# A hybrid encoder step on one Trainium2 core: the router of each token tile moved between the steps of the output projection, and ScalarE's work reordered where the running streams begin

## The chip, the cores and the metric

The kernel runs on one core of one Trainium2 chip. The metric is the device time of one execution in microseconds (us), the median of several runs. Everything is float32; large products are split into a high and a low part that TensorE takes as three float32r matmuls.

## What is computed

The reference is one layer over 512 prompt tokens and 8 running streams of 16 tokens, 640 tokens of width 1024. Cut to what matters here:

```python
x = x + concat(ao, go) @ w_out                 # ao: attention heads, go: gated linear attention
h = rms_norm(x, gain2)
g_logits = h @ w_group + b_group               # 4 groups
e_logits = h @ w_erouter + b_erouter           # 32 experts
# top group, top two experts in it, softmax weights
y = y + combine[:, e] * (silu(h @ w_gate[e]) * (h @ w_up[e])) @ w_down[e]
```

The attention of the prompt sees its own keys; that of a stream sees 512 cached keys and its 16 new ones.

## The kernel before

The 640 tokens are five tiles of 128 rows: tiles 0 to 3 are the prompt, tile 4 holds the eight streams. Each engine has one program, written out by hand, and the engines meet at semaphores: `then_inc` counts up, `wait_ge` holds the engine's queue until the count is reached. An engine works its instructions off in the order in which they are written, so a wait holds back all that stands behind it.

The place of the change begins where the prompt's attention ends (about 300 us) and ends where the mixture of experts begins (about 415 us):

- **The streams.** For each stream b the key cache and the value cache arrive in three buffers (SyncE, L505 and L513). TensorE computes scores (`d_scores`, L2007), VectorE the negated maximum (`d_max`, L1401), ScalarE two exponentials (`d_exps`, L931 and L933), VectorE a small table of factors (`d_comb`, L1410), TensorE transposes and combines (`d_pt`, L2023), ScalarE copies the result out of PSUM (`d_pts`, L942 and L943), TensorE multiplies with the values (`d_pv`, L2034). The loop runs over b with TensorE at score b, transpose b-2 and product b-3 in one turn.
- **The weights of the output projection** are halved into high and low parts between the streams' steps: `wo_high` (ScalarE, L790, 2048 columns at a time) and `wo_low` (VectorE, L1237). Both halves must be there before the first projection of this stage.
- **Projection of the attention part.** `a_step(s)` stands for three steps of tile i = s // 3: transposes of the mixed heads (TensorE L2052), split into high and low (`a_high` on ScalarE L954, `a_low` on VectorE L1417), and two projections of 512 columns, 12 matmuls each (L1955 to L1957). VectorE adds each half to the residual X (`a_add`, L1435). Steps 0 to 6 stand in the streams' turns, 7 to 14 behind them.
- **Router of tile i.** Eight transposes of X (`h2_tr`, TensorE L2093), two copies out of PSUM (`h2_out`, ScalarE L995), sum of squares (`sumsq`, VectorE L1467), root (`std_out`, ScalarE L1000), reciprocal and logits (`logits`, VectorE L1472 and L1475), the router's eight matmuls of 36 columns (`router`, TensorE L2104). `hn_out` (ScalarE L1007) writes the normed tile into one of two buffers `hn`, and GpSimd stores it to memory (L683), from where the experts gather their rows. `sumsq` writes its squares, which nobody reads, into the same buffer: for tile i of 2 and more it waits until the store of tile i-2 has landed (`st_hn`).
- **Choice of experts.** `pick` and `place` on VectorE for tiles 0 to 2, then for 3 and 4, with rank matmuls on TensorE, make the list of rows. GpSimd waits for the list and for all five stores, then gathers 128 rows for each of 16 pairs of experts (L712).
- **Experts.** Each has 3 MB of weights, in six buffers. SyncE loads experts 0 to 2 when the last stream's product is done (L516 and L519), 3 and 4 when the last projection is done, and the sixth when the first two gathers have landed; the others wait for a buffer.

ScalarE's `osq`, four squares and a root for the prompt's heads, needs another table of functions than the exponentials; each change of table is an instruction of its own (ACT_TABLE_LOAD). Two places say what sets the order around the change:

```python
            def sumsq(i):
                dve.wait_ge(x2_ready, 2 * NT + 2 * i + 2)
                if i >= 2:
                    dve.wait_ge(st_hn[i % 2], 16 * (i // 2))
```

```python
            sp.wait_ge(out_done, 4 * NT)
            for e in (3, 4):
                gate_up_of(e)
                down_of(e)
```

Of the kernel before, what the change touches and what calls it, by code (L numbers as in the profile page):

```python
# [24 lines left out]
P = 128  # L25
D = 1024
DC = D // P
NT = 5
NP = 4
CHUNK = 64  # L30
NB = 8
# [41 lines left out]
def build(nc, x, cache_kt, cache_v, state, w_main, w_ga, w_a2b, w_out, cols, k_gain, lam, w_r, b_r,  # L73
          w_gu, w_dn, y_out, k_out, v_out, sp_out, ss_out, hn_dram, ye_dram):
    ctx = ExitStack()
    with ctx:
# [653 lines left out]
        def _(act):  # L730
# [235 lines left out]
            d_exps(1)  # L966
            osq(NP - 1)
# [14 lines left out]
            for h in range(H):  # L982
                ins = act.activation(junk[:, h, :], bank[5][:, h * P:(h + 1) * P], ACT.Square,
                                     accum_out=sso[:, NP, h:h + 1])
            ins.then_inc(o_sq, 1)
            act.wait_ge(o_sq, NT)
            act.activation(ro[:, NP, 0:H], sso[:, NP, 0:H], ACT.Sqrt, bias=epsc[:, 0:1],
                           scale=1.0 / DV).then_inc(ostd, 1)

            def h2_out(i):  # L990
                for q in range(2):
# [87 lines left out]
        def _(dve):  # L1079
# [363 lines left out]
            d_max(0)  # L1443
            turn(NI + 2)
            d_max(1)
            d_comb(0)
            g_step(NS - 1)
            dve.wait_ge(ostd, 2)
            dve.reciprocal(ro[:, 0:NP, 0:H], ro[:, 0:NP, 0:H]).then_inc(ro_ready, 1)
            dve.wait_ge(x2_ready, 2 * NT)  # L1450
            for b in range(2, NB + 3):
                if b < NB:
                    d_max(b)
                if 5 <= b:
                    a_step(b - 5)
                if 1 <= b <= NB:
                    d_comb(b - 1)
                if b in (2, 3):
                    wo_low(1, b - 2)
# [844 lines left out]
```

## Time and profile before

| | |
|---|---|
| median of 3 runs | 695.02 us (694.23 to 702.57) |
| profiled execution, its own time | 696.28 us |
| its span in the trace | 694.5 us |
| mean granted TensorE clock | 0.922 of full |
| PE busy | 572.1 us (82%) |
| VectorE (DVE), ScalarE (ACT), GpSimd (POOL) busy | 251.4, 191.7, 88.2 us |
| moved by DMA | 166.46 MB, mean 240 GB/s |

The span runs from the first to the last instruction; 1.8 us of the execution's time lie outside it. A long busy time of an engine alone says little here: first TensorE sets the pace, then a web of short waits between engines, then the loading of the experts' weights.

### The profile page before, as it was taken

What the parts mean: (1) busy time and instruction counts of PE and PEld (TensorE: products, weight loads), DVE (VectorE), ACT (ScalarE), POOL (GpSimd) and SP (SyncE); (2) the same over time, 40 slices, a digit from 0 to 9 for tenths busy, and PEclk for the clock granted to TensorE, in tenths of its full rate; (3) what the DMA queues carried; (4) which work ended last, traced back from release to release, by engine and by line L of the source; (5) the groups of instructions that cost most, each with busy time, mean ns of one, the idle gap of its engine ahead of it and who ended that gap; (6) DMA issues with size and microseconds to landing.
All of it is one profiled execution on the core that took longest, in us unless ns stands there. A gap on an engine that the chain in (4) does not pass through costs nothing.

```text
span 694.5 us, 8437 instructions
## 1 busy us (share of the span) xinstructions
PE 572.1 (82%) x3375; PEld 377.7 (54%) x3375; DVE 251.4 (36%) x536; ACT 191.7 (28%) x439; POOL 88.2 (13%) x124
## 2 busy tenths in 40 slices
PE   5999999999989889769978837999968787878730
PEld 4878787777878667647866733444423333333200
DVE  3732347743593566535332671011100000100006
ACT  4441725232324444544332220111101111111110
POOL 4000000011862100010000111112111111110010
PEclk9999999999999899998997957999989999999885
DMA  8211221011343850068467286999999999999338
GB/s 300 68 62 60 96 88 61 1 62 61 121 176 135 333 212 1 1 255 322 152 267 319 98 376 225 424 423 427 422 424 425 423 425 424 426 424 428 144 138 357
DMA packets 24344, 166.46 MB, mean 240 GB/s; under 512 B 4752, under 2 KB 5328, under 8 KB 11120
## 3 DMA queue, kind: packets, MB, share of 16 engines
q1 hardware_dynamic: 17264, 146.36, 52.6%
q0 software_dynamic: 6320, 16.92, 6.3%
q10 hardware_dynamic: 720, 2.62, 0.9%
q8 instruction: 28, 0.46, 0.3%
q14 instruction: 12, 0.10, 0.0%
HBM read 154.74 MB, written 17.43 MB: 248 GB/s over the span
## 4 chain that ended last, share of the span: by engine, by line
PE 58%; DMA 24%; DVE 5%; ACT 5%; issue 4%; POOL 2%; SPq 1%; POOLq 0%; ACTq 0%; DVEq 0%
DMA egu<-in_w_gu 18%; PE twin L2183 11%; PE twin L1696 7%; PE twin L1698 7%; PE twin L1697 7%; PE twin L2203 3%; PE twin L1955 3%; PE twin L1956 3%; PE twin L1957 3%; DMA yg<-ye_dram 2%; PE twin L2034 2%; DMA hn_dram<-hn 1%; DVE xsT L1631 1%; DMA X<-in_x 1%; PE twin L2023 1%
## 5 line engine op out<-in xcount | busy, mean ns | idle before, releaser
L2183 PE MATMUL twin<-egu,xsT 128*64 128x512 f32 x512 | 130.0, 666 | 39.9 <-DMA egu<-in_w_gu 34.1
L2183 PEld LDWEIGHTS twin<-egu,xsT 128*64 128x64 f32 x512 | 46.4, 152 | 113.4 <-issue 113.4
L1696 PE MATMUL twin<-wH,hH 128*128 128x512 f32 x240 | 97.5, 406 | 0.0
L1698 PE MATMUL twin<-wH,hL 128*128 128x512 f32 x240 | 94.0, 392 | 0.0
L1697 PE MATMUL twin<-wL,hH 128*128 128x512 f32 x240 | 93.9, 391 | 0.0
L1637 DVE TENSOR_TENSOR hs<-sil,twin 128x256 f32<-128x256 f32 x16 | 6.7, 421 | 166.3 <-ACT sil L1034 166.3
L2203 PE MATMUL twin<-edn,hTs 128*64 128x512 f32 x256 | 58.1, 592 | 1.1 <-ACT hTs L1038 1.1
L1034 ACT ACTIVATE sil<-twin 128x256 f32<-128x256 f32 x16 | 6.1, 384 | 169.9 <-PE twin L2183 169.9
L1696 PEld LDWEIGHTS twin<-wH,hH 128*128 128x128 f32 x240 | 45.4, 189 | 10.7 <-issue 1.8
L1698 PEld LDWEIGHTS twin<-wH,hL 128*128 128x128 f32 x240 | 45.2, 188 | 9.9
L1697 PEld LDWEIGHTS twin<-wL,hH 128*128 128x128 f32 x240 | 45.4, 189 | 8.4
L1101 DVE SCALAR_TENSOR_TENSOR wL<-win,colt,wH 128x512 fp32r<-128x512 f32 x48 | 40.3, 901 | 5.4 <-ACT wH L742 5.4
L2203 PEld LDWEIGHTS twin<-edn,hTs 128*64 128x64 f32 x256 | 21.5, 137 | 34.1 <-issue 32.8
L1631 DVE TENSOR_TENSOR xsT<-twin,colt 128x512 f32<-128x512 f32 x32 | 20.7, 686 | 50.1 <-PE twin L2172 50.1
L712 POOL DMA_INDIRECT xs<-hn_dram,idx x16 | 16.1, 1007 | 177.9 <-ACT ysb L1049 153.1
L742 ACT ACTIVATE wH<-win,colt 128x512 fp32r<-128x512 f32 x48 | 30.7, 716 | 9.1 <-DMA win<-in_w_main 9.1
L1049 ACT ACTIVATE ysb<-twin 128x512 f32<-128x512 f32 x32 | 17.4, 595 | 49.5 <-PE twin L2203 49.5
L879 ACT ACTIVATE E<-twin,nm 128x128 f32<-128x128 f32 (+3 forms) x32 | 16.6, 524 | 30.4 <-DVE nm L1326 30.4
L2172 PEld LDWEIGHTS twin<-ident,xs 128*128 128x128 f32 x128 | 14.4, 146 | 18.7 <-issue 12.2
L639 POOL TENSOR_TENSOR zV<-zK 128x512 f32<-128x512 f32 x5 | 5.3, 1053 | 145.2 <-ACT zK L766 145.2
L2172 PE MATMUL twin<-ident,xs 128*128 128x128 f32 x128 | 18.4, 289 | 6.5 <-DMA xs<-hn_dram,idx 6.5
L1955 PE MATMUL twin<-wH,mixH 128*128 128x512 f32 x40 | 19.7, 492 | 4.4 <-DVE mixL L1351 2.4
(312 smaller groups left out, 823.4 us busy)
## 6 DMA issues: line engine op xcount, KB each, us to landing
egu<-in_w_gu SPq DMA_DIRECT2D x32, 2048.0 KB, 35.1
edn<-in_w_dn SPq DMA_DIRECT2D x32, 1024.0 KB, 39.2
win<-in_w_main SPq DMA_DIRECT2D x12, 1024.0 KB, 5.0
Kc<-in_cache_kt SPq DMA_DIRECT2D x8, 1024.0 KB, 9.9
Vc<-in_cache_v SPq DMA_DIRECT2D x8, 1024.0 KB, 6.9
X<-in_x SPq DMA_DIRECT2D x10, 512.0 KB, 8.1
yg<-ye_dram SPq DMA_DIRECT2D x5, 1024.0 KB, 9.1
hn_dram<-hn POOLq DMA_DIRECT2D x5, 512.0 KB, 2.9
```

The costliest lines, as they stand in the source:

```text
L742: act.activation(wH[k][:, o], win[k][:, o], ACT.Copy, scale=g1[:, 4 * k + s:4 * k + s + 1]).then_inc(wH_ready, 1)
L1101: dve.scalar_tensor_tensor(out=wL[k][:, o], in0=win[k][:, o], scalar=g1[:, 4 * k + s:4 * k + s + 1], in1=wH[k][:, o].bitcast(F32), op0=ALU ...
L1631: dve.tensor_tensor(xsT[q][:, 4 * hf:4 * hf + 4, :], bank[hf][:, :].rearrange("p (c s) -> p c s", c=4), bc(g2[:, 4 * hf:4 * hf + 4], [P, 4 ...
L1696: pe.matmul(bank[i][:, :], hH[:, d, i, :], wH[k][:, cs], start=(d == 0), stop=False)
L1697: pe.matmul(bank[i][:, :], hH[:, d, i, :], wL[k][:, cs], start=False, stop=False)
L1698: ins = pe.matmul(bank[i][:, :], hL[:, d, i, :], wH[k][:, cs], start=False, stop=(d == DC - 1))
L1955: pe.matmul(out, xH[i % 2][:, c, :], w_high, start=(c == 0), stop=False)
L1956: pe.matmul(out, xH[i % 2][:, c, :], w_low, start=False, stop=False)
L1957: ins = pe.matmul(out, xL[i % 2][:, c, :], w_high, start=False, stop=(c == H - 1))
L2172: ins = pe.transpose(bank[hf][:, c * P:(c + 1) * P], xs[q][:, (4 * hf + c) * P:(4 * hf + c + 1) * P], ident[:, :])
L2183: ins = pe.matmul(bank[2 + q][CAP * j:CAP * j + CAP, :], xsT[q][:, c, j * CAP:(j + 1) * CAP], egu[places[j]][:, c, :], start=(c == 0), sto ...
L2203: ins = pe.matmul(bank[4 + 2 * q + hf][CAP * j:CAP * j + CAP, :], hTs[q][:, f, j * CAP:(j + 1) * CAP], edn[places[j]][:, f, hf * 512:(hf + ...
```

## The change

It moves instructions and alters a few waits; no instruction of arithmetic is added or removed.

1. **ScalarE where the streams begin.** The copy-out of stream 0 (`d_pts(0)`) and the exponentials of stream 2 come ahead of `osq(3)` and its root. Copies-out stand one turn earlier in the loop, `wo_high` and VectorE's `wo_low` one turn later (b in 3 and 4 in place of 2 and 3), behind `d_pts` where they stood ahead of it.
2. **Tile 0's router in the streams' turns.** TensorE's `h2_tr(0)` goes into the turn b = 8, `router(0)` into b = 9, VectorE's `sumsq(0)` into b = 8.
3. **Interleaving.** Behind the streams the projections of the next tile are placed between the router's steps, so that a router matmul comes at least one projection after the transposes that it needs.

```diff
             d_exps(1)
+            d_pts(0)
+            d_exps(2)
             osq(NP - 1)
...
-            for b in range(2, NB + 3):
+            for b in range(3, NB + 2):
                 if b in (5, 8):
                     a_high((b - 5) // 3)
                 if b < NB:
                     d_exps(b)
-                if b in (2, 3):
-                    wo_high(1, b - 2)
-                if 2 <= b < NB + 2:
-                    d_pts(b - 2)
-            a_high(2)
-            act.wait_ge(d_pv_done, NB)
...
+                d_pts(b - 2)
+                if b in (3, 4):
+                    wo_high(1, b - 3)
...
+            h2_out(0)
             std_out(0)
-            h2_out(0)
+            a_high(2)
+            stream_squares()
+            h2_out(1)
+            std_out(1)
+            hn_out(0)
             a_high(3)
-            std_out(1)
-            h2_out(1)
-            hn_out(0)
+            hn_out(1)
+            h2_out(2)
+            std_out(2)
             a_high(4)
-            hn_out(1)
-            std_out(2)
-            h2_out(2)
             hn_out(2)
+            h2_out(3)
             std_out(3)
-            h2_out(3)
             hn_out(3)
+            h2_out(4)
             std_out(4)
-            h2_out(4)
             hn_out(4)
```

`stream_squares` is the four squares and the root of the streams' heads, which stood behind `a_high(2)` before. On VectorE:

```diff
+            for b in range(3, NB + 3):
...
+                if b in (3, 4):
+                    wo_low(1, b - 3)
+                if b == NB:
+                    sumsq(0)
+            logits(0)
...
             a_step(6)
-            stream_ao()
+            sumsq(1)
+            stream_copy()
             a_step(7)
+            stream_norm()
+            a_step(9)
+            logits(1)
             a_step(8)
-            sumsq(0)
-            a_step(9)
-            logits(0)
+            sumsq(2)
             a_step(10)
-            sumsq(1)
-            logits(1)
+            a_step(11)
             a_step(12)
-            a_step(11)
-            sumsq(2)
             sumsq(3)
             logits(2)
             pick(0, LATE[0])
             a_step(13)
-            logits(3)
             a_step(14)
             sumsq(4)
+            logits(3)
             place(0, LATE[0], 1)
```

And on TensorE, whose projections and routers behind the streams then read:

```diff
+                if b == NB:
+                    h2_tr(0)
+                if b == NB + 1:
+                    router(0)
+
+            h2_tr(1)
             a_step(7)
+            a_step(9)
+            router(1)
             a_step(8)
-            h2_tr(0)
-            a_step(9)
-            router(0)
-            h2_tr(1)
             a_step(10)
-            router(1)
+            h2_tr(2)
+            a_step(11)
             a_step(12)
-            a_step(11)
-            h2_tr(2)
             router(2)
             h2_tr(3)
             a_step(13)
+            a_step(14)
             router(3)
-            a_step(14)
             ranks(1)
             h2_tr(4)
             router(4)
```

On ScalarE, where the streams begin (E and enew are a stream's exponentials, PT its copy-out, junk the squares of `osq`, wH and woH the high halves of `wo_high`), the kernel before has:

```order
L894 ACTIVATE junk,sso<-zQ 128x128 x3
L969 ACT_TABLE_LOAD
L969 ACTIVATE ro<-sso,epsc 128x4x4 [waits o_sq]
L931 ACT_TABLE_LOAD [waits cb_ready,pt_done]
L931 ACTIVATE E,ds<-twin,nm 128x512 [waits nm_ready]
L933 ACTIVATE enew,ds<-twin,nm 128x16
L790 ACTIVATE wH<-win 128x2048 [waits out_done,ld_win0]
L942 ACTIVATE PT<-twin 128x512 [waits o_done,d_pt_done]
L943 ACTIVATE PT<-twin 128x128
```

and the changed kernel in the same place:

```order
L942 ACTIVATE PT<-twin 128x512 [waits o_done,d_pt_done]
L943 ACTIVATE PT<-twin 128x128
L931 ACTIVATE E,ds<-twin,nm 128x512 [waits cb_ready,pt_done,nm_ready]
L933 ACTIVATE enew,ds<-twin,nm 128x16
L894 ACTIVATE junk,sso<-zQ 128x128 [waits ao_ready]
L894 ACTIVATE junk,sso<-zQ 128x128 x3
L971 ACT_TABLE_LOAD
L971 ACTIVATE ro<-sso,epsc 128x4x4 [waits o_sq]
L931 ACT_TABLE_LOAD [waits cb_ready,d_pt_done]
L931 ACTIVATE E,ds<-twin,nm 128x512 [waits nm_ready]
L933 ACTIVATE enew,ds<-twin,nm 128x16
L942 ACTIVATE PT<-twin 128x512 [waits o_done,d_pt_done]
```

The first copy-out (PT) and one pair of exponentials moved ahead of the squares and of both table loads; the first `wo_high` moved behind the second copy-out, which is the last row shown.

On VectorE behind the streams, at the sums of squares of tiles 2 and 3 (ISA hn,ss is `sumsq`, Lg the logits, X an addition to the residual, mixL an `a_low`), the kernel before has:

```order
L1467 ISA hn,ss<-X 128x1024 [waits mT_done,x2_ready]
L1467 ISA ss 128x1
L1472 RECIPROCAL r<-st 128x1 [waits std1]
L1475 SCALAR_TENSOR_TENSOR Lg<-twin,r,br 128x36 [waits rstd1,lg_done]
L1423 SCALAR_TENSOR_TENSOR mixL<-twin,ag,mixH 128x4x32 [waits mH_ready]
L1423 SCALAR_TENSOR_TENSOR mixL<-twin,ag,mixH 128x4x32 x3
L1435 TENSOR_TENSOR X<-X,twin 128x512 [waits out_done]
L1467 ISA hn,ss<-X 128x1024 [waits st_hn0,x2_ready]
L1467 ISA ss 128x1
L1467 ISA hn,ss<-X 128x1024 [waits st_hn1,x2_ready]
```

and the changed kernel:

```order
L1463 SCALAR_TENSOR_TENSOR Lg<-twin,r,br 128x36 [waits rstd1,lg_done]
L1441 TENSOR_TENSOR X<-X,twin 128x512 [waits out_done]
L1455 ISA hn,ss<-X 128x1024 [waits st_hn0,x2_ready]
L1455 ISA ss 128x1
L1441 TENSOR_TENSOR X<-X,twin 128x512 [waits out_done] x2
L1429 SCALAR_TENSOR_TENSOR mixL<-twin,ag,mixH 128x4x32 [waits mH_ready]
L1429 SCALAR_TENSOR_TENSOR mixL<-twin,ag,mixH 128x4x32 x3
L1455 ISA hn,ss<-X 128x1024 [waits st_hn1,x2_ready]
L1455 ISA ss 128x1
L1460 RECIPROCAL r<-st 128x1 [waits std1]
```

The sum of squares that waits for the first store (`st_hn0`) now stands ahead of two additions and of the streams' `a_low`.

## Rows read from the trace of the kernel before

**Rows 1.** Busy time by stretch: us, each engine (x instructions), granted clock, DMA share, GB/s
```profile
327.00:352.60 25.60, 25.58 (x327) 19.86 (x325) 6.20 (x16) 5.60 (x17) 0.00 (x0) 1.00 0.39 148
352.60:397.80 45.20, 35.97 (x183) 30.93 (x183) 19.42 (x59) 14.53 (x32) 4.04 (x6) 0.85 0.63 256
440.00:642.00 202.00, 168.00 (x770) 70.54 (x766) 22.65 (x40) 24.36 (x53) 25.18 (x25) 0.93 1.01 424
```

**Rows 2.** Chain that ended last, 340 to 425 us: start, us, what
```profile
403.91 10.09 DMA hn_dram<-hn
...
414.86 4.16 DMA xs<-hn_dram,idx
```

**Rows 3.** Timeline of TensorE: start, us, line, operation, [idle before <- releaser]
```profile
313.71 2.05 PE L2023 MATMUL twin<-Cb,E 128*128 128x128 f32 x8 [5.76 <-ACT PT L943]
...
326.45 0.50 PE L1955 MATMUL twin<-wH,mixH 128*128 128x512 f32 x1
...
354.14 0.50 PE L1955 MATMUL twin<-wH,mixH 128*128 128x512 f32 x1 [1.56 <-DVE mixL L1417]
...
359.72 1.03 PE L2093 MATMUL twin<-ident,X 128*128 128x128 f32 x8
...
375.20 1.98 PE L2104 MATMUL twin<-wr,h2T 128*128 128x36 f32 x16 [3.22 <-ACT h2T L995]
```

**Rows 4.** Timeline of ScalarE
```profile
308.79 1.28 ACT L931 ACT_TABLE_LOAD   x1
310.08 0.69 ACT L931 ACTIVATE E<-twin,nm 128x512 f32<-128x512 f32 x1
...
311.01 1.90 ACT L790 ACTIVATE wH<-win 128x2048 fp32r<-128x2048 f32 x1
312.81 0.59 ACT L942 ACTIVATE PT<-twin 128x512 f32<-128x512 f32 x1
...
352.62 0.69 ACT L954 ACTIVATE mixH<-twin,ag 128x512 fp32r<-128x512 f32 x1 [5.22 <-PE twin L2052]
...
355.65 0.30 ACT L987 ACTIVATE ro<-sso,epsc 128x4 f32<-128x4 f32 x1
...
361.99 1.06 ACT L995 ACTIVATE h2T<-twin 128x512 f32<-128x512 f32 x2
```

**Rows 5.** Timeline of VectorE
```profile
312.94 2.37 DVE L1237 TENSOR_TENSOR wL<-win,wH 128x2048 fp32r<-128x2048 f32 x1 [1.72 <-ACT wH L790]
315.24 0.69 DVE L1401 TENSOR_REDUCE nm<-twin 128x1 f32<-128x528 f32 x1
...
387.52 0.17 DVE L1501 TENSOR_REDUCE gmax<-Lg 128x3 f32<-128x12 f32 x1
...
393.13 0.69 DVE L1435 TENSOR_TENSOR X<-X,twin 128x512 f32<-128x512 f32 x1
...
397.77 1.22 DVE L1467 CUSTOM_DVE_ANT_0 hn<-X 128x1024 f32<-128x1024 f32 x1
...
412.97 0.17 DVE L1612 SCALAR_TENSOR_TENSOR idx<-twin,none 128x17 int32<-128x17 f32 x1
```

**Rows 6.** The tile hn: durations of one in ns (min/median/max), and its stores
```profile
L1007 ACT ACTIVATE hn<-X,r x5: 1146/1148/1162, 375.0 to 402.5; 128x1024 f32<-128x1024 f32 x5
...
DMA to landing us min/median/max: 2.9/2.9/10.1
```

**Rows 7.** Timeline of SyncE: issues of the experts' loads
```profile
352.09 0.33 SPq L516 DMA_DIRECT2D egu<-in_w_gu  x1
...
397.04 0.33 SPq L516 DMA_DIRECT2D egu<-in_w_gu  x1
```

**Rows 8.** DMA queues from 408 to 412 us: packets, MB, share of 16 engines
```profile
q1 hardware_dynamic: 85, 1.34, 79.3%
q0 software_dynamic: 84, 0.34, 20.9%
```

**Rows 9.** DMA issues of the whole run: number, median us to landing
```profile
ye_dram<-ysb,dst POOLq DMA_INDIRECT x16, 14.4
```

More of the change, by code:

```diff
@@ L975, in _ @@
                     d_exps(b)
-                if b in (2, 3):
-                    wo_high(1, b - 2)
-                if 2 <= b < NB + 2:
-                    d_pts(b - 2)
-            a_high(2)
-            act.wait_ge(d_pv_done, NB)
[L982 to L988, printed above, removed]
+                d_pts(b - 2)
+                if b in (3, 4):
+                    wo_high(1, b - 3)
             def h2_out(i):
+                if i == 0:
+                    act.wait_ge(d_pv_done, NB - 2)
                 for q in range(2):
@@ L1441, in a_step @@
                     a_add(s // 3, s % 3 - 1)
[L1443 to L1459, printed above, removed]
             def sumsq(i):
@@ L1476, in logits, with stream_copy, stream_norm @@
                                          in1=br[:, :], op0=ALU.mult, op1=ALU.add).then_inc(lg_ready, 1)
-            def stream_ao():
+            d_max(0)
+            turn(NI + 2)
+            d_max(1)
+            d_comb(0)
+            g_step(NS - 1)
+            d_max(2)
+            d_comb(1)
+            dve.wait_ge(ostd, 2)
+            dve.reciprocal(ro[:, 0:NP, 0:H], ro[:, 0:NP, 0:H]).then_inc(ro_ready, 1)
+            dve.wait_ge(x2_ready, 2 * NT)
+            for b in range(3, NB + 3):
+                if b < NB:
+                    d_max(b)
+                if 5 <= b:
+                    a_step(b - 5)
+                if b <= NB:
+                    d_comb(b - 1)
+                if b in (3, 4):
[3 more added lines that the diff above has]
+            logits(0)
+            def stream_copy():
                 dve.wait_ge(o_sq, NT)
                 dve.tensor_copy(z(C_Q, NP), bank[5][:, :]).then_inc(ao_ready, 1)
+            def stream_norm():
                 dve.wait_ge(ostd, 3)
@@ L2069, in a_step @@
                 project_out(bank[7 if i < 2 or hf == 0 else 4][:, :], i, hf, 0, out_done)
-            turn(NI + 1)
-            d_scores(0)
-            turn(NI + 2)
-            d_scores(1)
-            for b in range(2, NB + 3):
-                if b < NB:
-                    d_scores(b)
-                if 2 <= b < NB + 2:
-                    d_pt(b - 2)
-                if b >= 3:
-                    d_pv(b - 3)
-                if b >= 4:
-                    a_step(b - 4)
             def h2_tr(i):
@@ L2100, in router @@
                     pe.wait_ge(lg_ready, i - 1)
+                elif i:
+                    pe.wait_ge(d_pt_ready, 2 * NB)
                 else:
                     pe.wait_ge(gains_ready, 1)
+                    pe.wait_ge(d_e_ready, 2 * NB)
                 for c in range(DC):
@@ L2138, in tables @@
                     ins.then_inc(tab_done, 1)
+            turn(NI + 1)
+            d_scores(0)
+            turn(NI + 2)
+            d_scores(1)
+            for b in range(2, NB + 3):
+                if b < NB:
+                    d_scores(b)
+                if 2 <= b < NB + 2:
+                    d_pt(b - 2)
+                if b >= 3:
+                    d_pv(b - 3)
+                if b >= 4:
+                    a_step(b - 4)
+                if b == NB:
[3 more added lines that the diff above has]
+            h2_tr(1)
             a_step(7)
+            a_step(9)
+            router(1)
             a_step(8)
-            h2_tr(0)
-            a_step(9)
-            router(0)
-            h2_tr(1)
             a_step(10)
-            router(1)
+            h2_tr(2)
+            a_step(11)
             a_step(12)
-            a_step(11)
-            h2_tr(2)
             router(2)
```

11 lines of the change are left out of this document (10 added, 1 removed).

## The prediction, made before the run

> **What bounds the kernel now.** I read the end first, then back to the place of the change. From 440 to 642 us the DMA engines are full (share 1.01, 424 GB/s) while TensorE waits for weights [rows 1]: that stretch lasts as long as its bytes take. It starts rigidly behind the first gathers, since SyncE's next loads wait for two gathers and for the buffers that the first pairs of experts free. The chain of waits shows what releases the first gather, at 414.86: the landing of the last store of `hn`, which took 10.09 us [rows 2], while the list of rows was ready at 413.1, 0.9 us sooner [rows 5]. So what counts is how soon the list and the stores are there, and whatever they gain the whole tail gains.
>
> Behind the last stream, from 352.6 to 397.8 us, TensorE is busy for 36.0 of 45.2 us, at a mean granted clock of 0.85 of 2.4 GHz [rows 1]. Its timeline shows why: projection, transposes, then a wait for a copy-out, 1.56 us before the projection of tile 2 and 3.22 us before the router of tile 1 [rows 3]. In the streams' turns before it, from 327 on, TensorE is busy for 25.58 of 25.60 us at full clock [rows 1]. At their beginning it waits 5.76 us for ScalarE's first copy-out [rows 3], which stands behind two table loads and a `wo_high` of 1.90 us [rows 4].
>
> I take two marks from before: t0 = 352.6, when ScalarE starts `a_high(2)` [rows 4], and S4 = 397.8, when VectorE starts the last sum of squares [rows 5]. From S4 to the gather it takes 17.1 us.
>
> **1. ScalarE where the streams begin: 0.6 us lost.** `d_pts(0)` no longer waits for the squares, so the 5.76 us go; but what is late next is the projection's weights. The two exponentials and copies put ahead delay the table loads' end from 310.1 to about 312.9 (0.85 for the copy, 0.95 for the exponentials, 1.05 waiting for the first transpose). Then follow one after the other, because each waits for the one before on the other engine: exponentials 0.95 and copy 0.85, `wo_high` 1.90, `wo_low` 2.37, maximum 0.69, exponentials 0.95, copy 0.85, `wo_high` 1.90, `wo_low` 2.3, maximum 0.69, and an `a_low` of 0.75 [rows 4, 5]: 14.2 us, so `a_step(1)` starts at 327.1 in place of 326.45 [rows 3]. The maximum of the next stream is queued behind each `wo_low` on VectorE, as before. SyncE's loads of keys and values are released no later than before and hide here. Bounds: 5.8 us gained if the weights don't decide, about 3 lost if more is late.
>
> The Trainium skill (ScalarE: Activation LUTs, section "What ACT_TABLE_LOAD costs") counts about 1.38 us of drain on top of 1.28 for each switch of tables. The trace has 1.28 and the exponential 0.01 us behind the load [rows 4]; by the page the two switches would end 2.8 us later and the time would be 688.7, but the row shows nothing of it.
>
> **2. Tile 0's router in the turns: 3.0 us lost on TensorE there.** TensorE is dense from 327 on, so eight transposes (1.03) and the router (1.98) have no cover [rows 3]. What they wait for is ready: ScalarE's two copies of `h2_out(0)` (1.06 [rows 4]) lie beside the projection between them.
>
> The granted clock is a cost that the order doesn't show. After the wait of 5.76 us four transposes ran at half clock, 2.05 us [rows 3]. The changed kernel spreads the same idle time over waits up to about 327, so the first dense block may run at half: between nothing and 3.4 us; I take 1.2, the first 2.4 us of a projection at half. So t0 becomes 352.6 + 0.6 + 3.0 + 1.2 = 357.4.
>
> **3. Interleaving: from t0 to S4 31 us in place of 45.2.** Two projections in a row take 5.6 us (354.14 to 359.72 [rows 3]). TensorE waits once more, some 0.7 us for `a_low(2)` beside the transposes of tile 1; after that each wait has a projection in front of it. Six projections (16.8), two routers (4.0), two sets of transposes of X (2.1) and two of heads (1.1) from 1.6 on end the last projection at t0 + 25.6. This is not the end of it: VectorE needs `pick` (5.6 us, 387.52 to 393.13 [rows 5]) after the sum of squares of tile 2 and 3, and these wait for stores.
>
> Now the stores. Before, three of five landed in 2.9 us; the last, issued at 403.9 beside the loads of experts 3 and 4 (issued from 397.04 on), took 10.1 [rows 2, 6, 7]. In the changed kernel the first three meet a load: experts 0 to 2 are issued 0.5 us before t0 as now [rows 7], and 9.4 MB at 424 GB/s with two stores among them last until about t0 + 25.8. ScalarE reaches the store of tile 0 after `a_high(2)` 0.69, squares and root (in all 2.05, the 3.33 us from 352.62 to 355.95 less a table load that now comes earlier), `h2_out(1)` 1.06, `std_out` 0.3, `hn_out(0)` 1.15 and 0.3 until the issue [rows 4, 6]: t0 + 5. At 10 us it lands at 15. Tile 1's store queues behind it: under load its queue moved 0.34 MB in 4 us [rows 8], so 0.52 MB take 6, until 21. `sumsq(3)` waits for this (it could start at 19). Then 1.22 for it, 1.4 for reciprocal and `hn_out(2)`, 0.3 to the issue: tile 2's store leaves at 24. `pick` ends at 28.3, two additions at 29.7, and `sumsq(4)` needs that store. It lands at 26.9 if it finds the engines free, at 34 if it meets load throughout. It is issued when the first load has under 2 us left, and experts 3 and 4 begin about 27, so it should find a gap: S4 between 29.7 and 34, taken at 31, nearer to the 2.9 row.
>
> The Trainium skill (DMA: Bandwidth & Descriptors, section "Anatomy of one DMA — SWDGE (gpsimd) path") gives 2.0 us plus the bytes at 436 GB/s for a transfer issued by GpSimd, 3.2 us by estimate for one store. Three of the five stores agree (2.9), the one under load doesn't (10.1) [rows 6]; taken for all of them the rule is the first rival below.
>
> **4. From S4 to the gather: 0.25 us lost.** `hn_out(3)` (1.15) now stands ahead of `h2_out(4)`, while the list instead of the last store releases the gather (0.9 gained). GpSimd's stores leave earlier, and experts 3 and 4 load while `pick` and `place` run, as before.
>
> **Sum.** S4 = 357.4 + 31 = 388.4, 9.35 earlier; less 0.25 is 9.1 us. The profiled execution took 696.28, its span plus 1.8, and would take 687.2; it was 1.26 above the median of the runs, so the forecast for the median is 695.02 - 9.1 = 685.9. Its own range: with no clock cost and S4 at 29.7, 683.4; with 3.4 and 34, 691.1. Two per cent, about what can be told from no change, is 13.9 us, so this counts as no change.
>
> **Rivals.**
> - *Stores land in 2.9 us even under load.* Then `sumsq(2)` and `sumsq(3)` never wait; the last projection ends at 25.6, additions follow `pick` at 27.6, and S4 is 27.7: 682.6. For it: three of five stores. Against: the one store that met a load [rows 2, 6], and that the two queues' packets alternate, 84 and 85 in 4 us, while the loads' are four times as large (1.34 MB to 0.34) [rows 8]. Chance 0.10.
> - *The weights don't hold the streams back.* Then the 5.76 us are gained, t0 is 6.4 earlier: 679.5. For it: the wait stands in the chain [rows 3]. Against: a `wo_low` has to end before `a_step(1)` and nothing shortens that chain. Chance 0.13.
> - *Slower: the stores take longer than that one did.* Two of them stand in a row before S4, and one in between, so S4 = 14 + 2x for a store of x us; it decides from x = 13.1 on. GpSimd's scatters on the same queue, all under full load, take 14.4 in the median [rows 9]: then S4 is 42.8, at 400.2 us, and the time 697.7. Against: they are scattered rows, and the plain store beside a load took 10.1. Chance 0.07.
>
> **How the numbers follow.** The forecast has a chance of 0.67, and 0.03 is left for what I don't see. Below 681.1 lie the second rival, a third of the first and the forecast's lower edge: faster by over 2% 0.20. Slower by over 2%, past 708.9, is only in what I don't see: 0.03. The rest, 0.77, is within 2%. The range of 8 in 10 goes from 678.0, which takes in the second rival with a little more, to 692.5, the forecast's upper bound and a little of what lies beyond.
>
> **What would show it.** Right: VectorE's third and fourth sums of squares wait for a DMA of `hn`, with stores of about 10 us after t0; `a_step(1)` starts near 327; TensorE is nearly dense from t0 to its last projection, at full clock; the gather starts near 405.8. Wrong: the copy-outs of the streams follow each other without the `wo_high` between them deciding (second rival), sums of squares that start behind an addition (first), or an S4 past 397 (third).

## The result, and the profile after

The changed kernel takes 683.55 us (median of 4 runs, 682.82 to 684.23), the kernel before, run beside it, 694.62 us. The ratio is 0.9863, 95% interval 0.9829 to 0.9896: 11.1 us less, which is within 2%. Here and below a ratio compares the fast executions alone, while medians and ranges take in all. The forecast was 685.9 us, 9.1 us less, with a range of 678.0 to 692.5.

The profiled execution took 683.54 us, its span 681.7. To compare executions I use one more mark, M: the start of ScalarE's exponentials of stream 0, just ahead of all that the change touches. It is at 299.44 us before and 299.82 in the changed kernel, and what lies ahead of it is nobody's gain or loss here. Timeline of ScalarE, changed kernel (start, us, line, operation, [idle before <- releaser]); the last row is the mark t0 of the prediction, at 352.62 before [rows 4]:

```profile
299.82 0.69 ACT L931 ACTIVATE E<-twin,nm 128x512 f32<-128x512 f32 x1 [4.90 <-DVE nm L1407]
...
310.18 1.28 ACT L971 ACT_TABLE_LOAD   x1
311.47 0.31 ACT L971 ACTIVATE ro<-sso,epsc 128x16 f32<-128x16 f32 x1
...
356.85 0.69 ACT L954 ACTIVATE mixH<-twin,ag 128x512 fp32r<-128x512 f32 x1 [4.34 <-PE twin L2064]
```

The busy time by stretch, columns as in [rows 1]: from 0.75 us ahead of t0 to 2.8 us behind S4, then t0 to the end of the last projection, then the place where the first projection of the turns runs.

```profile
356.10:390.00 33.90, 28.96 (x177) 25.03 (x170) 19.72 (x60) 12.23 (x29) 3.52 (x6) 0.92 0.97 398
356.85:381.35 24.50, 23.81 (x139) 20.48 (x137) 13.25 (x37) 10.77 (x27) 2.92 (x5) 1.00 0.99 402
326.00:330.00 4.00, 3.30 (x8) 2.67 (x9) 1.12 (x4) 1.69 (x6) 0.00 (x0) 0.57 0.54 223
```

Behind t0 TensorE is now busy 29.0 of 33.9 us (36.0 of 45.2 before), and the DMA share there is 0.97 in place of 0.63. Up to the end of its last projection it is nearly dense, and at full clock. Its timeline, where the waits of [rows 3] stood:

```profile
314.40 1.06 PE L2019 MATMUL twin<-Kc,qbd 128*32 128x512 f32 x8 [3.53 <-DMA Kc<-in_cache_kt]
...
326.70 0.79 PE L1967 MATMUL twin<-wH,mixH 128*128 128x512 f32 x1 [2.73 <-DVE mixL L1423]
...
358.38 0.50 PE L1967 MATMUL twin<-wH,mixH 128*128 128x512 f32 x1 [0.69 <-DVE mixL L1423]
...
385.53 1.97 PE L2091 MATMUL twin<-ident,X 128*128 128x128 f32 x8 [1.75 <-DVE X L1441]
390.71 3.63 PE L2105 MATMUL twin<-wr,h2T 128*128 128x36 f32 x16 [3.21 <-ACT h2T L989]
```

From 358.38 until the last projection ends it doesn't wait at all: of the 1.56 us of before 0.69 are left, and the 3.22 are gone. The waits of VectorE have moved to DMA. Its timeline (the first three rows are the sums of squares of tiles 2, 3 and 4; the last is the list of rows, at 412.97 before [rows 5]):

```profile
371.73 1.23 DVE L1455 CUSTOM_DVE_ANT_0 hn<-X 128x1024 f32<-128x1024 f32 x1 [4.63 <-DMA hn_dram<-hn]
...
376.77 1.23 DVE L1455 CUSTOM_DVE_ANT_0 hn<-X 128x1024 f32<-128x1024 f32 x1 [1.28 <-DMA hn_dram<-hn]
...
387.20 1.23 DVE L1455 CUSTOM_DVE_ANT_0 hn<-X 128x1024 f32<-128x1024 f32 x1 [1.73 <-DMA hn_dram<-hn]
...
404.01 0.17 DVE L1624 SCALAR_TENSOR_TENSOR idx<-twin,none 128x17 int32<-128x17 f32 x1
```

S4, the last of the three, is at 387.20, t0 + 30.35. The chain that ended last goes through two of these stores (start, us, what):

```profile
363.71 1.16 ACT hn L1001
364.87 0.29 issue
365.16 11.48 DMA hn_dram<-hn
376.77 1.23 DVE hn L1455
378.11 1.16 ACT hn L1001
379.27 0.28 issue
379.56 7.50 DMA hn_dram<-hn
387.20 1.23 DVE hn L1455
```

The view of the tile `hn` has for the five stores, where before it had 2.9, 2.9 and 10.1 [rows 6]:

```profile
DMA to landing us min/median/max: 7.5/10.2/11.5
```

GpSimd's first gather now waits for the list, not for a store:

```profile
405.13 1.10 POOL L712 DMA_INDIRECT xs<-hn_dram,idx  x1 [10.83 <-DVE idx L1624]
```

So the 12.8 us of the two spans (694.5 and 681.7) divide as follows. M is 0.38 later. The gather comes 105.31 us after M in place of 115.42: 10.11 gained. From the gather to the end of the span it is 276.57 us in place of 279.64: 3.07 gained, of which 2.95 are one group of matmuls, the gate and up product of the last pair of experts, during which the granted clock is 0.70 before and 1.00 changed. TensorE's timeline, before and changed:

```profile
647.74 10.04 PE L2183 MATMUL twin<-egu,xsT 128*64 128x512 f32 x32 [4.15 <-DMA egu<-in_w_gu]
```

```profile
638.14 7.09 PE L2200 MATMUL twin<-egu,xsT 128*64 128x512 f32 x32 [2.45 <-DMA egu<-in_w_gu]
```

### The profile page after: what moved, and what is told of

It is laid out like the page before. It is cut to its first block, busy times and chain, and to the rows that moved or that the text cites. A ratio compares the mean times of both kernels' runs of the same rounds, so it can differ in the third digit from the quotient of the medians.

```text
span 681.7 us, 8438 instructions
## 1 busy us (share of the span) xinstructions
PE 563.9 (83%) x3375; PEld 373.0 (55%) x3375; DVE 250.5 (37%) x536; ACT 191.3 (28%) x439; POOL 88.2 (13%) x124
## 4 chain that ended last, share of the span: by engine, by line
PE 55%; DMA 26%; DVE 6%; ACT 6%; issue 3%; POOL 2%; SPq 1%; POOLq 0%; ACTq 0%; DVEq 0%
DMA egu<-in_w_gu 19%; PE twin L2200 11%; PE twin L1708 7%; PE twin L1710 7%; PE twin L1709 7%; PE twin L2220 4%; DMA hn_dram<-hn 3%; PE twin L1967 3%; DMA yg<-ye_dram 2%; PE twin L1968 2%; PE twin L1969 2%; DMA X<-in_x 1%; DVE xsT L1643 1%; PE twin L1903 1%; POOL zK L646 1%
## 5 line engine op out<-in xcount | busy, mean ns | idle before, releaser
L2200 PE MATMUL twin<-egu,xsT 128*64 128x512 f32 x512 | 128.4, 659 | 38.6 <-DMA egu<-in_w_gu 32.8
L1710 PEld LDWEIGHTS twin<-wH,hL 128*128 128x128 f32 x240 | 45.2, 188 | 9.8
```

What stands on the lines that cost most here:

```text
L1710: ins = pe.matmul(bank[i][:, :], hL[:, d, i, :], wH[k][:, cs], start=False, stop=(d == DC - 1))
L2200: ins = pe.matmul(bank[2 + q][CAP * j:CAP * j + CAP, :], xsT[q][:, c, j * CAP:(j + 1) * CAP], egu[places[j]][:, c, :], start=(c == 0), sto ...
```

## The experiments

My theory: the interleaving (part 3) gains, and what then sets S4 are the stores of `hn` under the loads of experts 0 to 2; part 1 is neutral but for the clock; part 2 costs TensorE what it holds. Rivals: parts 1 and 2 carry the gain; the waits for stores are slack; the load isn't what makes the stores slow. The marks of all profiled executions (us, worked out from the timelines; "tail" is from the first gather to the end of the span, "last pair" its gate and up product). A mark comes from one execution. The medians were taken at four times, and the kernel before, run beside them, took 694.62 us (first two rows), 692.55 (one tile after the other, part 2 undone, part 1 undone, own scratch), 692.51 (changed again, two experts first, late loads, three edits) and 693.11 (the rest), so times are compared by their ratios:

| kernel | M | t0 - M | S4 - t0 | gather - M | tail | last pair | profiled | median |
|---|---|---|---|---|---|---|---|---|
| before | 299.44 | 53.18 | 45.15 | 115.42 | 279.64 | 10.04 | 696.28 | 694.62 |
| changed | 299.82 | 57.03 | 30.35 | 105.31 | 276.57 | 7.09 | 683.54 | 683.55 |
| changed, again | 298.72 | 55.61 | 29.24 | 102.80 | 278.68 | 8.49 | 682.08 | 683.67 |
| one tile after the other | 298.86 | 55.61 | 44.04 | 116.62 | 280.22 | 10.08 | 697.56 | 695.53 |
| part 2 undone | 298.95 | 53.02 | 33.22 | 104.18 | 280.07 | 8.78 | 685.25 | 687.96 |
| part 1 undone | 299.87 | 55.73 | 29.22 | 103.68 | 279.15 | 8.61 | 684.74 | 681.84 |
| part 3 alone | 297.99 | 52.97 | 37.48 | 108.39 | 279.72 | 8.65 | 687.96 | 687.36 |
| own scratch | 295.87 | 55.61 | 27.29 | 100.83 | 276.80 | 7.09 | 675.57 | 681.73 |
| two experts first | 295.93 | 55.62 | 28.45 | 102.37 | 278.50 | 7.09 | 678.73 | 684.68 |
| late loads | 299.60 | 57.05 | 27.30 | 102.70 | 289.60 | 8.78 | 693.85 | 690.16 |
| three edits | 300.00 | 55.82 | 27.30 | 101.94 | 279.56 | 10.00 | 683.46 | 679.48 |
| three edits, again | 296.48 | 55.58 | 27.29 | 101.83 | 279.49 | 8.64 | 679.74 | 679.74 |
| and last store free | 296.56 | 55.61 | 27.29 | 99.41 | 282.13 | 8.79 | 680.07 | 680.21 |

### The changed kernel again

No edit.

> The changed kernel once more, unaltered, as the yardstick for the runs beside it and for how far its executions scatter. My theory of the tail (from the first gather to the end of the span 276.6 us, of which 7.1 are the last pair's gate and up product at full clock, and 3 us more where that product falls into a low clock): the time is 683 to 687, each execution near one of two levels some 2 to 3 us apart, and in the profiled one the tail less the last pair's product is 269.5 within 1.5. Rival (the shorter tail of the first profile belongs to the change): every execution within 1 us of 683.5.

683.67 us (682.08 to 687.35, 6 runs), ratio 0.9884 (0.9842 to 0.9926). The tail less the last pair's product is 270.19, as expected; the product took 8.49 us this time. The rival, a shorter tail by the change, falls: the same kernel has either. The two levels of time that I expected don't appear, the six times lie spread. The gather starts 1.13 us behind the list of rows, 1.12 in the first profile; here it is the last store that is named as its releaser, so list and store come nearly together. t0 is 1.42 us nearer to M than in the first profile, and the stretches show why: the low clock, which met the first projection there (0.57 from 326 to 330), lies between 314 and 318 here, behind a wait of 3.52 us for a key cache. The first profile has that wait too (3.53 us), with the clock at 1.00 behind it.

```profile
326.00:330.00 4.00, 4.00 (x31) 2.65 (x30) 0.35 (x2) 0.61 (x2) 0.00 (x0) 1.00 0.30 117
314.00:318.00 4.00, 4.00 (x54) 3.20 (x50) 2.49 (x2) 1.48 (x1) 1.08 (x2) 0.62 1.01 426
```

### One tile after the other

TensorE's order (VectorE's and ScalarE's likewise):

```diff
-            h2_tr(1)
             a_step(7)
+            a_step(8)
             a_step(9)
-            router(1)
-            a_step(8)
+            h2_tr(1)
             a_step(10)
-            h2_tr(2)
+            router(1)
+            a_step(12)
             a_step(11)
-            a_step(12)
+            h2_tr(2)
             router(2)
```

> The changed kernel with parts 1 and 2 kept, but behind the last stream the order of before on TensorE, VectorE and ScalarE: each tile's projection, transposes and router one after the other. My theory (the interleaving is what gained): from t0, where ScalarE copies the heads of tile 2, to S4, the last sum of squares, it takes again 42 to 45 us in place of 30.35, the gather starts 10 to 12 us later than 405.13, and the time is 693 to 697. Rival (parts 1 and 2 carry half of the gain): t0 stays at about 356.9 and the time rises by 3 to 6 us only, to 687 to 690. If the 3 us that the tail gained beyond the gather belong to the interleaving, the tail from the gather's start to the end of the span is 3 us longer as well; if they are chance, it may be either length.

695.53 us (692.94 to 698.02, 12 runs), ratio 1.0044 (1.0019 to 1.007): without part 3 nothing of the gain is left, and 0.4% is lost. S4 - t0 is 44.04, nearly the 45.15 of before, and the gather comes 11.3 us after that of the first profile of the changed kernel (both from M), released by a store as before:

```profile
415.48 1.10 POOL L712 DMA_INDIRECT xs<-hn_dram,idx  x1 [10.29 <-DMA hn_dram<-hn]
```

### Part 2 undone

```diff
-                if b == NB:
-                    h2_tr(0)
-                if b == NB + 1:
-                    router(0)
 
-            h2_tr(1)
+            h2_tr(0)
             a_step(7)
+            router(0)
+            h2_tr(1)
             a_step(9)
             router(1)
```

ScalarE's copies and VectorE's logits of tile 0 go back with them; VectorE's `sumsq(0)` stays in the turns.

> The changed kernel without part 2: tile 0's transposes and router stand behind the streams again, the transposes ahead of the projection of tile 2 and the router behind its first half; the rest of the interleaving is kept. My theory: t0 is 3.0 us earlier (the TensorE time of transposes and router), but TensorE does that work after t0, and the store of tile 0 leaves about 2 us later, so S4 and the gather come 2 us later (0 to 4) and the time is 684 to 687.5. Rival (the stores don't set S4, TensorE does): S4 and the time as in the changed kernel, within 0.5 us. Second rival (the move only cost): the 3.0 us come back and the time is 680 to 681.

687.96 us (684.47 to 691.25, 12 runs), ratio 0.9937 (0.9909 to 0.9965). t0 is 2.6 us earlier, S4 - t0 4.0 us longer than in the second profile of the changed kernel, the gather 1.4 later. The direction is the theory's; the median lies 0.5 us above its range and some 4 above that of the changed kernel, while the marks show 1.4. The interval lies apart from the first one of the changed kernel and overlaps the second a little. The profiled execution, 685.25, is one of the quicker. Why the others are slower the next run suggests.

### Part 3 alone

Part 2 undone as above, and part 1 as below.

> The kernel before with the interleaving alone: parts 1 and 2 undone, so that only the order behind the last stream is that of the changed kernel. My theory (the interleaving gains what is gained, parts 1 and 2 move it by less than 2 us together): the gather comes 103 to 105.5 us after the first exponentials of the streams, in place of 115.4 before and 102.8 to 105.3 changed, and the time is 684 to 689. Rival (the interleaving pays only with tile 0's router out of the way): the gather at 108 or later and a time of 690 and more.

687.36 us (679.65 to 691.70, 6 runs), ratio 0.9858 (0.9798 to 0.9918), too wide an interval to tell it from the changed kernel or from part 2 undone. The time is within my range, but the gather comes at M + 108.39, where the rival put it, 4.2 us behind the run with part 2 alone undone, though t0 is the same. Most of the difference is one store. With part 2 undone the third store left at 379.24 and SyncE's load of expert 3 at 379.75, 0.5 us behind it; the last sum of squares met no wait. The view of the DMA issues, 378 to 387 us, has for this one store (KB each, us from issue to landing):

```profile
hn_dram<-hn POOLq DMA_DIRECT2D x1, 512.0 KB, 3.7
```

With part 3 alone both left together (SyncE, then GpSimd):

```profile
378.83 0.33 SPq L516 DMA_DIRECT2D egu<-in_w_gu  x1
```

```profile
378.78 0.53 POOL L683 DMA_DIRECT2D hn_dram<-hn  x1 [15.22 <-ACT hn L999]
```

and VectorE waited until the store landed. The view of the DMA issues, 376 to 384 us, and VectorE's timeline:

```profile
hn_dram<-hn POOLq DMA_DIRECT2D x1, 512.0 KB, 9.5
```

```profile
388.44 1.23 DVE L1453 CUSTOM_DVE_ANT_0 hn<-X 128x1024 f32<-128x1024 f32 x1 [3.76 <-DMA hn_dram<-hn]
```

With part 2 kept, the third store leaves 1.8 to 2.3 us ahead of that load (379.56 and 381.33 in the first profile) and landed in 7.5 and 6.3; it leaves sooner behind t0, while the load of experts 0 to 2 still runs (DMA share 0.92 from 379 to 381, against 0.10 from 378 to 380 with part 2 undone). So part 2, which costs TensorE 2.6 us ahead of t0, takes the third store out of a race with the load of expert 3. That this race is what scatters the executions without part 2 over 7 and 12 us fits, but only two of them were profiled; it is not shown.

### Part 1 undone

```diff
             d_exps(1)
-            d_pts(0)
-            d_exps(2)
             osq(NP - 1)
...
-            for b in range(3, NB + 2):
+            for b in range(2, NB + 2):
...
+                if b in (2, 3):
+                    wo_high(1, b - 2)
                 d_pts(b - 2)
-                if b in (3, 4):
-                    wo_high(1, b - 3)
```

On VectorE the maximum of stream 2, the factors of stream 1 and `wo_low` go back likewise.

> The changed kernel without part 1: where the streams begin ScalarE and VectorE work in the order of before, the first copy-out behind the squares and a weight copy. My theory: the wait of 5.76 us before the first heads' product comes back, but the first projection of the turns starts within 0.5 us of 326.7, because the weights' chain decides; the half clock at the first projection goes (1.3 us back), so t0 is 0 to 1.8 us earlier and the time is 682 to 684. Rival (the first copy-out holds the streams back): the first projection starts 4 to 6 us later and the time is 687.5 to 690.

681.84 us (679.01 to 684.74, 6 runs), ratio 0.9843 (0.9809 to 0.9876), the changed kernel's within the intervals. TensorE's timeline, and the second `wo_low` in VectorE's:

```profile
314.12 2.04 PE L2031 MATMUL twin<-Cb,E 128*128 128x128 f32 x8 [5.76 <-ACT PT L943]
...
326.87 0.50 PE L1963 MATMUL twin<-wH,mixH 128*128 128x512 f32 x1
```

```profile
319.24 2.29 DVE L1241 TENSOR_TENSOR woL<-woin,woH 128x2048 fp32r<-128x2048 f32 x1 [2.34 <-ACT woH L790]
```

The same instruction in the changed kernel:

```profile
323.07 2.29 DVE L1243 TENSOR_TENSOR woL<-woin,woH 128x2048 fp32r<-128x2048 f32 x1 [3.00 <-ACT woH L790]
```

The wait of 5.76 us is back, and the first projection starts at M + 27.00, with part 1 at M + 26.88. The rival falls: part 1 as a whole gains nothing. It doesn't follow that the wait cost nothing. Without part 1 the weights are ready at M + 21.7, 5.3 us ahead of the first projection, and TensorE goes from the end of the wait to that projection without a pause: its own chain behind the wait decides. With part 1 the weights are ready at M + 25.5, because `wo_high` and `wo_low` stand one turn later, and the projection waits 2.73 us for the `a_low` queued behind them. One wait was exchanged for another. What it would bring to take the first away and leave the weights where they were, no run shows.

### A scratch of its own for the sums of squares

```diff
+        sq = [at("sq0", 5 * KW, D), at("sq1", 17 * KW, D)]
...
-                if i >= 2:
-                    dve.wait_ge(st_hn[i % 2], 16 * (i // 2))
-                else:
-                    dve.wait_ge(mT_done, NT)
-                dve.tensor_tensor_reduce(out=hn[i % 2][:, :],
+                dve.wait_ge(mT_done, NT)
+                dve.tensor_tensor_reduce(out=(hn[i] if i < 2 else sq[i // 4])[:, :],
```

> The changed kernel, but VectorE's sums of squares of tiles 2 to 4 write their unused product to a scratch of their own (the free places of the exponentials and of the low parts of the heads) in place of the buffers of hn, so that VectorE no longer waits for the stores; ScalarE's scaling into hn still does. SyncE's loads of experts 3 and 4 wait for the fourth sum of squares too. My theory (the stores under the load of experts 0 to 2 set S4): no sum of squares waits for a DMA, S4 falls from t0 + 30.35 to about t0 + 25.6 to 27, the gather starts 3.5 to 5 us earlier, and the time is 678.5 to 680. Rival (the projections and the pick set S4, the waits were slack): S4 and the time stay within 1 us. Second rival (the gain is lost again because the last store then releases the gather): S4 earlier by 4 us, the gather by under 2, and a time of 681.5 to 683.

681.73 us (675.57 to 681.93, 7 runs), ratio 0.9842 (0.9811 to 0.9874). No sum of squares waits any more, though the stores are as slow (8.5 to 11.3 us):

```profile
361.77 1.22 DVE L1454 CUSTOM_DVE_ANT_0 sq<-X 128x1024 f32<-128x1024 f32 x1
...
370.05 1.22 DVE L1454 CUSTOM_DVE_ANT_0 sq<-X 128x1024 f32<-128x1024 f32 x1
...
378.77 1.22 DVE L1454 CUSTOM_DVE_ANT_0 sq<-X 128x1024 f32<-128x1024 f32 x1
```

S4 falls to t0 + 27.29, the gather to M + 100.83, 2.0 and 4.5 us before the two profiles of the changed kernel. So the waits are on the path. SyncE's added wait delays nothing: expert 3 is issued at t0 + 24.47, in the changed kernel at t0 + 24.48. In time a gain is not shown: the ratio is within the intervals of the changed kernel, whose median is 1.8 us higher but was taken beside a kernel before that was 2.1 us slower; I had 3.5 to 5. The profiled execution, 675.57, is by 4 us the quickest of the seven.

### Late loads

```diff
-            for e in range(3):
-                gate_up_of(e)
-                down_of(e)
             sp.wait_ge(out_done, 4 * NT)
-            for e in (3, 4):
+            for e in range(5):
```

> The changed kernel, but SyncE loads all of experts 0 to 4 only behind the last projection, so that the first three stores meet no load. My theory: these land in about 2.9 us, no sum of squares waits for one, S4 falls from t0 + 30.35 to t0 + 25.6 to 27.5 (as with a scratch of its own); the last two stores and the gathers meet the load (10 us and more), and 15.7 MB at 424 GB/s keep the DMA engines until about 418, some 9 us later than now, so that the tail starts late and the time is 5 to 11 us higher than the changed kernel beside it. Rival (the stores' 7.5 to 11.5 us are not the load's doing): the first three stores take as long as now and S4 stays at t0 + 30.

690.16 us (688.17 to 693.85, 12 runs), ratio 0.996 (0.9931 to 0.9988). The first stores land as they did before, at least three of five in 2.9 us:

```profile
DMA to landing us min/median/max: 2.9/2.9/11.0
```

No sum of squares waits, S4 is t0 + 27.30, as with a scratch of its own, and the tail is 289.60: the loads come too late, and the first gather runs beside them, 9.2 us from its issue to TensorE's transposes in place of 4.2. The median is 6.5 us above that of the changed kernel beside it. The rival (slow whatever the load) falls: with the load gone the store is quick, with it back it is slow.

### Two experts first

```diff
-            for e in range(3):
+            for e in range(2):
...
-            for e in (3, 4):
+            for e in (2, 3, 4):
```

> The changed kernel, but SyncE loads only experts 0 and 1 behind the streams (6.3 MB), and expert 2 together with 3 and 4 behind the last projection. My theory (the load makes the stores slow): the first two stores still meet the load and land in 9 to 11 us, the third meets none and lands in about 3 us; the second lands a little earlier, so S4 comes 2 to 3 us earlier; the last two stores and the gathers now meet a load that lasts until about 404, which gives back 0 to 2 us. The time is 0 to 3 us lower than the changed kernel beside it. Rival (stores are slow whatever the load): S4 unchanged and the time the same or, with the loads later, up to 3 us higher.

684.68 us (678.73 to 685.36, 7 runs), ratio 0.9889 (0.9851 to 0.9927): no gain. The third store did land in 2.9 us and S4 - t0 is 28.45, but the second landed no sooner: two experts' loads still lasted until it was down. The gathers then met the load of three experts (TensorE waited 7.94 us for the first in place of 5.72). Of S4 I had the sign right and the size too large; the time, said to be 0 to 3 us lower, is 1.0 us higher in the median, within the intervals.

### Three edits together

Part 1 undone, the scratch, and on ScalarE:

```diff
-            hn_out(3)
             h2_out(4)
+            hn_out(3)
             std_out(4)
```

> The changed kernel with three edits: part 1 undone, VectorE's sums of squares of tiles 2 to 4 into a scratch of their own, and ScalarE's copy-out of the last tile's transposes ahead of its scaling of tile 3. My theory: t0 1.3 us earlier, S4 at t0 + 27.3 in place of 30.35, and the router of tile 4 some 0.5 us sooner behind it, so the gather comes about 5 us earlier than in the changed kernel beside it, and the time is 4 to 6 us lower. Rival (the last store then releases the gather, as it did with part 1 undone alone): the gather comes 2 to 3 us earlier only, released by a store, and the time is 2 to 3 us lower.

> The three edits once more, unaltered, as the yardstick for the fourth: 678 to 682 us, the first gather again released by a store of hn, 101 to 102.5 us after the first exponentials of the streams.

679.48 (674.47 to 683.46) and 679.74 us (679.36 to 680.53), 6 runs each; ratios 0.9791 (0.9745 to 0.9836) and 0.9793 (0.9753 to 0.9832), some 4 us under the changed kernel (683.67 beside the first of them) and the best version found. The list of rows starts at M + 98.3 and 98.4, 104.2 and 101.7 in the two profiles of the changed kernel, but the gather goes at M + 101.9 and 101.8: the rival's mechanism, with the time that I had given to my own. GpSimd's timeline of the second of them:

```profile
385.92 0.53 POOL L685 DMA_DIRECT2D hn_dram<-hn  x1 [2.50 <-ACT hn L1001]
398.31 1.10 POOL L714 DMA_INDIRECT xs<-hn_dram,idx  x1 [11.86 <-DMA hn_dram<-hn]
```

The last store left at 385.92 and took 11.5 us, under the loads of experts 3 and 4.

### And the last store free of the load

```diff
             for e in (3, 4):
+                if e == 4:
+                    sp.wait_ge(st_hn[0], 3 * 16)
+                    sp.wait_ge(st_hn[1], 2 * 16)
                 gate_up_of(e)
```

> The three edits together (part 1 undone, own scratch, last copy-out first) and a fourth: SyncE loads expert 4 only when the last store of hn has landed; expert 3 as before. My theory (in the three edits alone the list of rows was ready 3.7 us ahead of the first gather, which waited for a store of 11 us under the loads of experts 3 and 4): the last store now meets the end of expert 3's load or no load and lands in 3 to 5 us, the list releases the gather, the gather comes 2 to 2.7 us earlier after the start of the streams than with three edits, and the time is about 2.5 us under that of the three edits beside it. Rival (the load of expert 4, 3 to 5 us later, holds the tail back by what the gather gains): the gather earlier, the rest of the tail longer, and the time within 1 us.

680.21 us (679.48 to 683.36, 6 runs), ratio 0.9807 (0.9765 to 0.9849), 0.5 us over the three edits beside it: the rival. The list releases the gather, 2.4 us sooner after M, but the gather itself now meets the load of expert 4. Here and with three edits, GpSimd issues it at 395.97 and 398.31, and TensorE's transposes begin at 402.35 and 402.76 (TensorE's timelines, this kernel first):

```profile
402.35 1.97 PE L2187 MATMUL twin<-ident,xs 128*128 128x128 f32 x8 [7.87 <-DMA xs<-hn_dram,idx]
```

```profile
402.76 1.97 PE L2184 MATMUL twin<-ident,xs 128*128 128x128 f32 x8 [8.22 <-DMA xs<-hn_dram,idx]
```

6.4 us in place of 4.45: 1.9 of the 2.4 us are gone at once, and the tail is 2.6 us longer. Here what stands beside the load pays, the store or the gather.

## Why the prediction was right, step by step

**The whole.** 9.1 us were forecast and 11.1 measured, 8.8 the second time, by the forecast's own mechanism. In the profiled execution the gather is at 405.13, forecast 405.8. From M to the gather 14.80 us were gained behind t0, 3.85 lost ahead of it and 0.84 behind S4, 10.11 in all; the forecast had 14.2, 4.8 and 0.25.

**Part 1, 0.6 lost: nothing lost.** In the changed kernel the weights' chain decides, as said: `a_step(1)` starts at M + 26.88, part 1 undone at M + 27.00. I had it 0.65 later, mostly because I added the whole of each copy-out where the next instruction starts before it ends (a `wo_high` starts 0.63 us behind the copy's start, not 0.85). Of the second way, the 5.76 us as a gain, nothing appeared, because part 1 itself puts the weights 3.9 us later; in the kernel before they had 5 us to spare. The table loads stand at 1.28 us with the root 0.01 us behind one of them. The Trainium skill (ScalarE: Activation LUTs, section "What ACT_TABLE_LOAD costs") adds about 1.38 us of drain to each switch; this trace too has none.

**The clock, 1.2 lost: 1.4 or nothing.** In the first profile the first projections ran at the lower clock as forecast (0.57), and t0 was 1.42 us later than in the second profile, where it ran at full clock. Of the seven profiles that contain part 1, t0 - M is 57.03 and 57.05 in two, 55.6 in four, and the one without part 2 is at the latter less 2.6. The 1.2, made of 2.4 us at half clock, came from no row: the first profile has 2.9 us at 0.50, the lower of the two levels, 1.2 of 2.4 GHz (326.7 to 329.6), the second none there. It is an either-or inside the bounds of nothing and 3.4, and a mean was taken. Of the row behind the 5.76 us the working misread one thing: it holds eight matmuls, not four, and the slow pace went on behind it to about 319.7.

**Part 2, 3.0 lost on TensorE: 2.6.** In the chain the eight transposes are 0.88 and the router 1.71 us; I had the durations of the timeline, which overlap with what follows. That this is a mere loss was wrong: behind t0 it is given back (from M to S4 it is 84.85 us in the second profile of the changed kernel and 86.24 with part 2 undone), and the third store gains a lead on the load (the runs without part 2).

**t0** came out at 356.85, forecast 357.4; with M's own 0.38 the sum of the three terms is 3.85 in place of 4.8.

**Part 3, t0 to S4 in 31 us: 30.35, and 29.24 the second time.** The single steps, as t0 plus: first store landed 15, measured 14.9 by the sum that waits for it; second 21, measured 19.8; third issued 24, measured 22.7, and landed, between 26.9 and 34, at 30.2. The scratch and the late loads both give 27.3 when stores don't decide; my first rival had 27.7. So of 30.35 and 29.24 some 3 and 2 us are the stores' doing. One step came out by luck. The third store was to find a gap, with under 2 us of the first load left and experts 3 and 4 about to start at 27. There was no gap: the DMA share is 0.92 from 379 to 381, and experts 3 and 4 were issued at 24.5. That the store took 7.5 us and not 10 put S4 beside the 31 taken. The gap is there in the run without part 2 (share 0.10 from 378 to 380), and its store took 3.7.

The Trainium skill (DMA: Bandwidth & Descriptors, section "Anatomy of one DMA — SWDGE (gpsimd) path") gives 3.2 us by estimate for such a store: the run without a load has 2.9, the runs beside one have mostly 6 to 13, for which the rule has no term.

**Part 4, 0.25 lost: 0.84 lost.** S4 to the gather is 17.93 us, 17.09 before. `h2_out(4)` behind `hn_out(3)` makes the router of tile 4 start 0.93 us later after S4 (1.15 foreseen), and the list as releaser gains 0.77 (0.9 foreseen). The missing term is the router itself: it ran 3.63 us at the lower clock (0.50 from 390.7 to 394.4), where before it took 2.94.

**The tail, said to gain what the gather gains: only within 3 us.** In eleven of the thirteen profiles the tail less the last pair's product is 269.5 to 271.4 us (the other two are the late loads and the last one, where the gather meets a load). The product takes from 7.09 to 10.08, by the clock that it meets (1.00 for 7.09, 0.83 for 8.49, 0.70 for 10.04). One kernel has either: 7.09 and 8.49 in the two profiles of the changed kernel, 10.00 and 8.64 in those of the three edits. The first profile of the changed kernel had the least, and that of before almost the most; 2.95 of the 12.8 us between the two spans are this and not the change. Against M the two profiles of the changed kernel gain 10.1 and 12.6 us up to the gather, and the medians 11.1 and 8.8: the forecast of 9.1 lies among them.

**The rivals.** Quick stores (0.10) and a start that isn't held by the weights (0.13) were shown not to be so in the changed kernel. The argument against the second, that nothing shortens the weights' chain, holds for this change, which makes that chain later. The slower one would have taken the whole gain at 13.1 us per store (14 + 26.2 behind the forecast t0 is 397.6, where S4 stood before); the two in the chain took 11.5 and 7.5.

Open stays why the medians follow the gather only roughly: with a scratch the gather is 2 to 4.5 us earlier, and no gain in time can be told from the scatter; with part 2 undone the gather is 1.4 us later, the median some 4. M differs by 4 us between profiles (295.87 to 300.00, by 3.5 between the two of the three edits), and the last pair's product by 3, more than most single edits are worth.

## What to carry to other kernels

When a schedule is tightened, ask what the transfers will meet: a store that is free where the engines are slow lands beside the next load once they are quick, and costs three times as much; a buffer that is shared only to hold an unread result turns that into a wait. A wait of 5.76 us in the middle of the chain went and nothing was gained, because the same edit made another chain (the weights) later: before a wait is counted as a gain, look at what the edit that removes it delays. And with a clock that falls at varying places, compare marks inside the trace, measured from a point ahead of the change, before the times of single executions are read.

## What the runs showed that I had not expected

- A store of 512 KB takes 2.9 us alone and mostly 6 to 13 beside loads of weights. Issued 0.5 us ahead of a load it took 3.7 us, issued with it 9.5: half a us decided over nearly 6.
- The lower clock comes at different places in two executions of one kernel (0.57 at 326 to 330 us, then 1.00 there and 0.62 at 314 to 318), the first time behind a wait of 2.73 us, the second behind one of 3.52, which the first execution had too without the clock falling. And one product of 32 matmuls took 7.09, 8.5 to 8.8, or 10.0 us.
- Moving a load out of a store's way put it in the gather's: 4.45 us became 6.4, and the time didn't change.
